# Seven buffers for u and eleven for v in the gather ring of a PEER mixer, instead of eight and ten

## What is computed

```
def _peer(xn, wq, subkeys, u, v):            # per chunk of 128 tokens
    q = (xc @ wq).reshape(T, 8, 2, 128)
    s = einsum('thpd,pkd->thpk', q, subkeys)
    s_top, i_top = top_k(s, 16)              # 16 keys per head and half
    cand = s_top[:, :, 0, :, None] + s_top[:, :, 1, None, :]
    best_s, pos = top_k(cand, 16)            # 16 experts per head: idx, 128 per token
    gate = softmax(best_s)
    u_sel = take(u, idx)                     # rows of 1024 float32
    act = gelu(einsum('thkd,td->thk', u_sel, xc))
    v_sel = take(v, idx)
    return einsum('thk,thkd->td', gate * act, v_sel)
```

## Time and profile before

| | us |
|---|---|
| median of 3 runs | 1798.77 (1796.46 to 1799.69) |
| the profiled execution | 1797.66 |
| its span, first to last instruction | 1795.7 |
| PE busy | 1525.6 (85%) |
| POOL busy | 1101.3 (61%) |
| DVE busy | 1027.0 (57%) |
| ACT busy | 387.9 (22%) |
| DMA | 687.11 MB, mean 383 GB/s |

### The profile page before, as it was taken

One profiled execution on the slowest core, in us unless ns is written; L12 is line 12 of the kernel. 1 busy time (PEld: TensorE's weight loads), 2 busy tenths in 40 slices (PEclk: granted clock), 3 DMA queues, 4 the chain that ended last, 5 costly groups with the idle time before them and its releaser, 6 DMA issues.

```text
span 1795.7 us, 13519 instructions
## 1 busy us (share of the span) xinstructions
PE 1525.6 (85%) x3952; PEld 672.4 (37%) x3952; DVE 1027.0 (57%) x2479; ACT 387.9 (22%) x965; POOL 1101.3 (61%) x1131
## 2 busy tenths in 40 slices
PE   4998879989988888999997768999989877767777
PEld 3755434443332333444442223444344322222222
DVE  6566854676566562444457775436446876544442
ACT  2222132221111140141312132133222221111110
POOL 4221576766665774656756775656656777766664
PEclk9999989989999999999999989999989999999999
DMA  9998899999999999999999999999999999999997
GB/s 375 399 388 285 285 336 395 393 409 399 404 404 406 406 409 389 399 403 407 404 402 408 410 367 367 403 401 409 394 407 407 366 391 340 392 365 370 365 375 275
DMA packets 214653, 687.11 MB, mean 383 GB/s; under 512 B 20883, under 2 KB 21557, under 8 KB 214582
## 3 DMA queue, kind: packets, MB, share of 16 engines
q0 software_dynamic: 158976, 578.88, 82.9%
q1 hardware_dynamic: 54544, 105.98, 15.7%
q10 hardware_dynamic: 1062, 1.40, 0.2%
HBM read 685.14 MB, written 1.05 MB: 382 GB/s over the span
## 4 chain that ended last, share of the span: by engine, by line
PE 40%; DMA 22%; POOL 17%; issue 9%; DVE 8%; another core or an unknown queue 3%; ACT 1%; DVEq 0%; POOLq 0%
PE pair L1010 20%; PE pair L180 13%; DMA net_u<-in_peer_u,net_cols 12%; POOL net_v L581 8%; POOL net_u L581 8%; DMA net_v<-in_peer_v,net_cols 4%; DVE net_u L1778 4%; DMA net_w<-in_b_w_qo 3%; PE pair L203 2%; PE pair L196 2%; DMA net_w<-in_kv_w 1%; DMA net_v<-in_ada_w 1%; PE pair L613 1%; PE pair L618 1%
## 5 line engine op out<-in xcount | busy, mean ns | idle before, releaser
L1010 PE MATMUL pair<-net_v,net_diags 128*128 128x512 f32 x2048 | 976.5, 612 | 161.4 <-DMA net_v<-in_peer_v,net_cols 91.6
L581 POOL DMA_INDIRECT net_v<-in_peer_v,net_cols x512 | 521.7, 1019 | 331.0 <-PE pair L1010 151.3
L581 POOL DMA_INDIRECT net_u<-in_peer_u,net_cols x512 | 517.4, 1011 | 224.8 <-issue 139.8
L1010 PEld LDWEIGHTS pair<-net_v,net_diags 128*128 128x128 f32 x2048 | 373.0, 192 | 709.0 <-issue 492.2
L1778 DVE SCALAR_TENSOR_TENSOR net_u<-net_u,pair 128x1024 f32<-128x1024 f32 x320 | 386.9, 1218 | 275.2 <-DMA net_u<-in_peer_u,net_cols 185.6
L180 PE MATMUL pair<-net_w,net_work 128*128 128x512 f32 x624 | 294.4, 611 | 22.5 <-DMA net_w<-in_b_w_qo 14.3
L1354 ACT ACTIVATE net_diags<-ident,net_cols 128x128 f32<-128x128 f32 x512 | 171.1, 392 | 657.8 <-DVE net_cols L1450 354.5
L1778 DVE SCALAR_TENSOR_TENSOR net_u<-net_u,net_x_tok 128x1024 f32<-128x1024 f32 x192 | 233.2, 1220 | 98.0 <-DMA net_u<-in_peer_u,net_cols 71.0
L180 PEld LDWEIGHTS pair<-net_w,net_work 128*128 128x128 f32 x624 | 119.7, 196 | 168.5 <-issue 160.7
L1450 DVE TENSOR_TENSOR net_cols<-net_cols,net_gate 128x4 f32<-128x4 f32 (+1 forms) x124 | 19.9, 161 | 129.8 <-ACT net_cols L1347 109.5
L225 POOL DMA_DIRECT2D net_u<-in_ada_w x46 | 24.8, 541 | 80.5 <-DVE net_sc L237 21.1
(11 more groups left out here) (243 smaller groups left out, 977.6 us busy)
## 6 DMA issues: line engine op xcount, KB each, us to landing
net_w<-in_peer_wq SPq DMA_DIRECT2D x12, 2048.0 KB
net_u<-in_ada_w POOLq DMA_DIRECT2D x46, 512.0 KB, 9.3
net_w<-in_ada_w SPq DMA_DIRECT2D x8, 2048.0 KB
net_w<-in_kv_w SPq DMA_DIRECT2D x8, 2048.0 KB
net_w<-in_b_w_qo SPq DMA_DIRECT2D x8, 2048.0 KB
net_v<-in_ada_w POOLq DMA_DIRECT2D x18, 512.0 KB, 12.6
net_u<-in_kv_ada_w POOLq DMA_DIRECT2D x16, 512.0 KB, 6.6
net_u<-in_peer_u,net_cols POOLq DMA_INDIRECT x512
```

The source lines that it names most:

```text
L581: eng.indirect_dma_start(slot, None, rows, bass.IndirectOffsetOnAxis(ap=idx[:, i, k:k + 1], axis=0)).then_inc(landed, 16)
L1010: mm = eng.matmul(acc[q % 2][:, at], diag[n % DIAGS][:, :], vb[n % V_SLOTS][:, at], start=(k == 0), stop=(k == SEL - 1))
```

## The change

One of the eight u buffers becomes the eleventh v buffer. The memory stays where it is: the last 1024 columns of `u_all` are now named `vb[10]`. Two numbers change, and with them the waits: u(n) waits for the dot product of tile n-7, v(m) for the sum of tile m-11, and `POOL_SHIFT` falls from 22 to 21. The lags between u and v in POOL's queue are as before. No instruction is added or taken away but a few semaphore instructions.

```
-    U_SLOTS = 8
-    V_SLOTS = 10
+    U_SLOTS = 7
+    V_SLOTS = 11
...
-        u_all, v_all = ph.sb("u", [P, U_SLOTS * D]), ph.sb("v", [P, V_SLOTS * D])
+        u_all, v_all = ph.sb("u", [P, 8 * D]), ph.sb("v", [P, 10 * D])
         ub = [u_all[:, n * D:(n + 1) * D] for n in range(U_SLOTS)]
-        vb = [v_all[:, n * D:(n + 1) * D] for n in range(V_SLOTS)]
+        vb = [v_all[:, n * D:(n + 1) * D] for n in range(10)] + [u_all[:, 7 * D:8 * D]]
```

## The result

The changed kernel takes 1819.18 us (median of 1814.00, 1816.14, 1822.22 and 1826.54) against 1799.23 us for the kernel before, run beside it. The ratio is 1.0107, 95% interval 1.0077 to 1.0138: it is slower, by some 20 us, and outside the range of the prediction (1780 to 1801).

The account below looks back on a forecast made before the run. It took the DMA engines as the limit where they never pause, and in the tail POOL's waits for PE's late reports as what starves them. -13.75 + 0 + 0 + 0 from 1797.66 gave 1783.9, as median 1785; range 1780 to 1801.

Parts of the forecast that it names:

- Part 1: In the tail, v(m) waiting for m-11 instead of m-10 shortens the groups of pauses, 13.75 us together.
- the tie to PE's own progress: The forecast case: in the tail, late reports come at PE's own progress, as at tile 434's start; 1785 us, chance 0.54.
- The term of 13.75 us: Tail gain: five groups of pauses shorter by 2.50 us each, the last by 1.25 us.
- 22 us of pause: DMA pause in the tail, from share 0.95 of a possible 1.03, taken as room for the gain.
- B: Rival: late reports tied to the standstill; tail pauses stay 5.4 us long, every 18 tiles instead of 17; 1797 us, chance 0.28.
- Part 2: u(n) waits for n-7 instead of n-8: nothing in the tail, up to 2.50 us per place before it; taken as 0.
- the cover: At u(384), a wait of 1.21 us for the last route swallows some 2 us of POOL's gain or loss before it.
- Part 3: The tail begins at u(384), when DVE has written the last route's indices; earlier POOL shifts of some 2 us add 0.
- Part 4: Roots one pair earlier in POOL's queue: between 0 and -3.92 us, taken as 0.
- Part 5: At weight loads, one more pair queued ahead of POOL's stop: 0 to 2.6 us each, taken as 0.
- rival C: The extra pair delays weights at both second-layer loads, 5.2 us at tile 345's scores, u(384) later than 1402; 1804 us, chance 0.18.

Follow-up runs that it names:

- e6: Kernel before with eight u buffers up to tile 255 and seven from 256 on, ten for v, roots as before: ratio 0.9993 to the kernel before.
- f2: Kernel before with seven u buffers throughout and ten for v, on a chip with prompt reports: ratio 1.0040 to the kernel before.
- e1: Changed kernel with ten v buffers instead of eleven, seven for u, the eighth u buffer unused: 1820.25 us, ratio 1.0078 to the kernel before.
- f1: The changed kernel itself, run again on a chip with prompt reports: ratio 1.0043 to the kernel before.
- e8: Kernel before with only the roots of the loop moved one pair of gathers earlier in GpSimd's queue: ratio 1.0005 to the kernel before.
- e5: Kernel before with seven u buffers up to tile 251 and eight from 252 on, ten for v: ratio 1.0057 to the kernel before.
- g1: Changed kernel with the last root of the start queued ahead of u(19) instead of u(20): ratio 1.0106 to the kernel before.
- e11: Kernel before, but from u(400) on GpSimd waits ahead of each eighth u gather until all issued gathers have landed: ratio 1.0490 to the kernel before.

## Why the prediction was wrong

**Part 1, the gain of 13.75 us in the tail: failed.** The step is the sentence "If that report still comes when PE starts on tile 434, POOL has issued one pair more by then, and each group of pauses is shorter by 2.50 us". The reading of the place was right: the pauses are there, on v gathers, 16 or 17 tiles apart, and the DMA engines run dry in them. What was wrong is the tie to PE's own progress. The term of 13.75 us measured nothing: from sum 400 to sum 511 it takes 302.1 us before and 303.1 after. The pause moves with the gathers: 5.4 us a group with eleven buffers, and all pauses from v(430) on are about as much with nine, ten, eleven and fourteen, 26.6 to 30.0 us. The room of "22 us of pause" was real, 28 us if the chips without pauses differ in nothing else, but a buffer is no handle on it. The prediction held the right rival, B, at 0.28, with half of the sign that came: pauses as long as before, but 16 to 17 tiles apart and not 18. Its price, 1797 us, lacks the loss of part 2 (the pauses that it multiplies add up to 30.2 us, not 29, which changes that price by less than 0.1 us). The rule of the Trainium skill that was quoted there (Perfetto Trace Analysis, section Optimization Strategy, and not the section that the prediction names), that such gaps can mean too few buffers, is not borne out for these gaps: four more buffers took none of them away.

**Part 2, the shorter lead of u at 0: failed for the first half, and this is the sign of the result.** It priced one hold, u(323), at up to 2.50 us, and covered all holds by one wait at u(384). For the second half that is right as far as can be measured (e6, 0.9993). The holds at the start were not looked at: each hold by a dot product falls one step earlier in the queue, and what is queued behind u(19) is not only a gather but a root for which PE stands. A step is one u and two v there, which GpSimd issues more slowly (1.15 to 1.87 us each), 5.4 us and not 2.50; the root is 4.7 us late, at a place at which PE is the bound, some 1160 us ahead of the cover. The bounds of part 2 counted one place at 2.50 us and were given no sum over the places. Seven for u and ten for v cost 1.0040 on a chip with prompt reports (f2) and 1.0078 on one with late reports (e1), against the 0 of this part. The other holds of the first half are on both kinds of chip: GpSimd's wait at u(38) is 14.0 us in f1 too. In the changed kernel's profile it grew from none to 13.4 us (the kernel before has 6.34 at u(39)), and the DMA share from 300 to 320 us fell from 0.96 to 0.77:

```profile
308.67 0.94 POOL L581 DMA_INDIRECT net_u<-in_peer_u,net_cols  x1 [13.40 <-DVE net_u L1778]
...
300.00:320.00 20.00, 20.00 (x60) 9.75 (x59) 14.12 (x53) 6.19 (x14) 9.50 (x7) 1.00 0.77 274
```

**Part 3, the tail begins with the route's indices: the step is right, its use was wrong.** It still does: the route of tile 384 is written at 1421.79 us and the gather goes at 1422.24. But the whole chain to it is 23.8 us late. "DVE works without a break at this point" says nothing of when it gets there.

```profile
1421.79 0.18 DVE L1435 TENSOR_SCALAR net_cols<-net_key 128x32 uint32<-128x32 f32 x1
```

**Part 4, the roots at 0: right** for the eight of the loop (e8, 1.0005). The root that counts was one of the start, which stands ahead of u(20) in both kernels and was not moved; what moved was the wait of the gather ahead of it.

**Part 5 and rival C, the weights: not seen.** u(384) did come later than 1402, as C said, but the weight piece on the chain that ended last is shorter than the 18.02 us of the earlier trace rows:

```profile
1115.89 16.57 DMA net_w<-in_b_w_qo
```

The second piece of the earlier trace rows is not on this chain, whose part ahead of 1115 us the profile puts down to no instruction. C had the side right and named the wrong mechanism; its 5.2 us at the second layer are not the loss of the first half.

**What the prediction could not know from one trace** is that the late reports come on some chips and not on others. It called them odd and built its one gain on them.

How the 1.07% divides on a chip with late reports stays open. e1 and e5 put most of it on the lead of u in the first half. The start's 4.6 us were taken back in g1, and the sums were 6.7 us late again at tile 48; the later holds, the late reports, the eleventh buffer of v and PE's clock were not taken apart there. The clock is a part that the prediction did not look at: over all executions it is 0.940 to 0.948 in g1 and 0.952 to 0.966 in the kernel before beside it, while with prompt reports f1 has 0.969 to 0.974 and the kernel before 0.968 to 0.979. Whether the lower clock lengthens the loss or only follows from the standstills is not shown. Whether g1's line takes back the 0.27% on a chip with prompt reports was not tried.

## What to carry to other kernels

A ring that gives up a buffer is held one step earlier at each place where its consumer stands; walk through every such place from the first tile on, and price not the gather that is held but whatever is queued behind it on that engine, above all a small operation for which another engine stands. A cover found late in a kernel covers nothing that moves the cover itself. Before a gain is built on a wait whose cause is unknown, vary the one quantity that is to shorten it: a ring four buffers longer in the tail would have shown in one run that these pauses do not follow it.

## What the runs showed of the hardware

The same program has two paces on different chips, 1799 to 1808 us on A, B and E and 1759 to 1760 us on C and D. The traces show a cause or a companion: 200 to 238 of 512 sums report promptly in the ten traces of A, B and E, 512 of 512 in all eight of C and D. Each chip was used at one time only, so chip and time are not told apart; and every execution on record has a granted clock, which is read from a recording, so no run shows whether the lateness comes with the recording.

In the traces with late reports there are places where PE starts its matmuls one by one, 2.1 us apart, while the DMA engines are full, and goes on when they run empty. The changed kernel around v(438), PE first and then the stretches of 2 us (the last two columns are DMA share and GB/s, the one ahead the granted clock, which falls to the lower level, 1.2 GHz, after PE has been idle for 4.7 of 6 us):

```profile
1613.32 0.59 PE L1010 MATMUL pair<-net_v,net_diags 128*128 128x512 f32 x1 [1.69 <-issue]
1615.42 0.59 PE L1010 MATMUL pair<-net_v,net_diags 128*128 128x512 f32 x1 [1.51 <-issue]
1617.53 9.10 PE L1010 MATMUL pair<-net_v,net_diags 128*128 128x512 f32 x14 [1.52 <-issue]
```
```profile
1614.00:1616.00 2.00, 0.58 (x1) 0.19 (x1) 0.69 (x2) 0.00 (x0) 0.00 (x0) 1.00 1.02 406
1616.00:1618.00 2.00, 0.48 (x2) 0.29 (x1) 1.23 (x2) 0.00 (x0) 0.00 (x0) 0.64 0.65 260
1618.00:1620.00 2.00, 2.00 (x3) 0.84 (x3) 1.31 (x3) 0.63 (x3) 1.23 (x2) 0.50 0.00 0
```

What holds PE then is not shown by any run; the two kernels made to ask it met a chip without late reports. Letting the DMA engines run empty cost twice the 3 us that e11's expectation gave it: 14 drains took 87 us, 6.2 us each.
